# Hybrid mixer and MoE layer: a new order of the mixer's work on four engines

## The reference, cut to what matters

```python
proj = xn @ w_in                       # 1024 -> 1792 columns, 14 column tiles of 128
ya = short_conv_mixer(a_b, a_c, a_x, conv_a_w)          # tiles 0..5
yb = pool_mixer(p_u, pool_w, pool_b, pool_scale)        # tiles 6, 7
yc = s5_mixer(s_u, ...)                                 # tiles 8, 9: bu = B u, h = scan(a, bu), y = C h + d u
yd = rglru_mixer(l_x, l_g, ...)                         # tiles 10..13
branch = einsum('bskw,kwd->bskd', stack(ya, yb, yc, yd), branch_w)
gates  = sigmoid(xn @ merge_gate_w + merge_gate_b)
merged = sum(gates * branch) ;  out = merged @ w_out
```

## Time and profile before

| what | value |
| --- | --- |
| median of 3 runs | 2529.59 us (2528.16 to 2534.01) |
| the profiled execution | 2537.29 us, its span 2535.6 us |
| PE, DVE, ACT, POOL busy in the span | 93%, 54%, 44%, 27% |
| granted TensorE clock, mean | 0.969 of full speed |
| mixer, from the start to the first merge matmul | 500 us |

### The profile page before, as it was taken

How to read it: one execution, slowest core, us unless ns; L and a number is a source line. 1 busy time by engine, 2 the same in 40 slices (tenths; PEclk the granted TensorE clock), 3 DMA queues, 4 the chain that set the end, 5 groups by cost and what they waited for, 6 DMA issues and landing times. The chain is left out here.

```text
span 2535.6 us, 33774 instructions
## 1 busy us (share of the span) xinstructions
PE 2359.7 (93%) x11388; PEld 1854.2 (73%) x11389; DVE 1369.4 (54%) x1967; ACT 1118.1 (44%) x1444; POOL 673.4 (27%) x514
## 2 busy tenths in 40 slices
PE   6979899799999999999999999499999999999991
PEld 5757777688888888888888887377667766677771
DVE  6888575634444444434443444655555556547565
ACT  4523333133333333333333332457666666567673
POOL 3821101100000000000000000077555756567771
PEclk9989999899999999999999999699999999999996
DMA  7864747343354435543463333379777978799987
GB/s 238 321 233 156 240 169 238 89 147 94 106 195 141 125 94 169 179 125 94 119 222 94 100 96 112 141 251 339 276 256 270 340 263 270 261 328 346 328 296 285
DMA packets 311869, 516.31 MB, mean 204 GB/s; under 512 B 33180, under 2 KB 211616, under 8 KB 295392
## 3 DMA queue, kind: packets, MB, share of 16 engines
q1 hardware_dynamic: 295312, 458.17, 51.4%
q0 software_dynamic: 16464, 56.90, 8.9%
HBM read 430.33 MB, written 84.68 MB: 203 GB/s over the span
## 5 line engine op out<-in xcount | busy, mean ns | idle before, releaser
L1496 PE MATMUL mrgps<-xn_hi,w_hi 128*128 128x512 f32 x1024 | 401.4, 392 | 6.7 <-DVE w_lo L1615 6.7
L1496 PE MATMUL mrgps<-xn_hi,w_lo 128*128 128x512 f32 x1024 | 399.5, 390 | 0.0
L1496 PE MATMUL mrgps<-xn_lo,w_hi 128*128 128x512 f32 x1024 | 399.5, 390 | 0.0
L1998 POOL TENSOR_TENSOR w_lo<-w_raw,w_hi 128x1024 fp32r<-128x1024 f32 x128 | 343.0, 2836 | 0.0
L2159 PE MATMUL exps<-w_hi,x_room 128*128 128x512 f32 x1024 | 330.4, 399 | 4.9 <-issue 4.3
L1427 ACT ACTIVATE gt<-mrgps,mb 128x512 f32<-128x512 f32 x128 | 88.3, 690 | 509.1 <-PE mrgps L1496 503.0
L1761 POOL MEMSET x_ident<- 128x128 f32 x1 | 0.2, 205 | 1109.1 <-POOLq L1223 1109.1
L1993 DVE TENSOR_TENSOR w_lo<-w_raw,w_hi 128x2048 fp32r<-128x2048 f32 x126 | 283.5, 2310 | 0.0
L1632 DVE SCALAR_TENSOR_TENSOR tmp<-gt,mrgps 128x512 f32<-128x512 f32 x96 | 66.0, 688 | 387.0 <-PE mrgps L1496 387.0
L1983 ACT ACTIVATE w_hi<-w_raw 128x2048 fp32r<-128x2048 f32 x128 | 239.1, 1921 | 8.4 <-DMA w_raw<-in_expert_w_dram 8.3
L2159 PEld LDWEIGHTS exps<-w_hi,x_room 128*128 128x128 f32 x1024 | 193.2, 189 | 65.1 <-issue 18.3
(11 more groups left out here) (427 smaller groups left out, 4114.5 us busy)
## 6 DMA issues: line engine op xcount, KB each, us to landing
w_raw<-in_expert_w_dram SPq DMA_DIRECT2D x192, 1024.0 KB, 10.1
w_raw<-in_merge_gate_w_dram SPq DMA_DIRECT2D x128, 512.0 KB, 4.0
win_hi<-w_in_parts SPq DMA_DIRECT2D x42, 512.0 KB, 3.6
win_lo<-w_in_parts SPq DMA_DIRECT2D x42, 512.0 KB, 4.9
w_raw<-in_branch_w_dram SPq DMA_DIRECT2D x128, 128.0 KB, 4.1
wout<-in_w_out_dram SPq DMA_DIRECT2D x64, 256.0 KB, 4.5
w_raw<-in_x_dram SPq DMA_DIRECT2D x16, 512.0 KB, 9.7
branch_rows<-in_x_dram SPq DMA_DIRECT2D x16, 512.0 KB, 5.8
```

The source lines that it names most:

```text
L1496: last = pe.matmul(bank[:], w[:, u % 2, kk], x, start=(kk == w_tiles[0] and j == 0), stop=(kk == w_tiles[-1] and j == 2))
L1998: eng.tensor_tensor(self.lo2[:, f], self.raw2[:, f], self.hi2[:, f].bitcast(F32), ALU.subtract).then_inc(self.split2, 1)
```

## The change

The computation is the same. Its parts:
- In chunk 1 `states_in` waits for ACT's copies of `toeplitz` only; the wait for the diagonal stands ahead of `states_out(0, 0)`.
- The order of the steps of chunks 1, 2 and 3 is written anew on PE, DVE and ACT, with tile 9 ahead of `glu(c - 1)` in chunks 2 and 3.
- The transposed x is stored in 4 pieces of 1 MB, each behind another weight load, and x is read in two pairs of pieces in place of four at once; two stores move.
- In chunk 0 the row scales are worked out in two halves (rows 0, 1 and rows 2, 3 of the four x pieces), DVE scales pieces 1 and 3 and ACT pieces 0 and 2, and ACT does the high parts of the first weight pieces later.

```diff
-            return f(*range(6)) + gates(c) + f(6, 7, 8) + glu(c - 1) + f(9, 10, 11) + (glu(c) if c == CH - 1 else [])
+            return f(*range(6)) + gates(c) + f(6, 7, 8, 9) + glu(c - 1) + f(10, 11) + (glu(c) if c == CH - 1 else [])
...
                     if i == 7:
                         store(0, c - 1, ya_full, ya)
+                    if i == (10 if c == 1 else 7):
                         store(1, c - 1, yb_full, pl)
...
-                    if i == 6 and c + 1 < CH:
-                        store_xT(c)
-                        load_x(c + 1)
+                    if 4 <= i < 8 and c + 1 < CH:
+                        store_xT(c, (i - 4,))
+                    if 8 <= i < 10 and c + 1 < CH:
+                        load_x(c + 1, (2 * i - 16, 2 * i - 15))
...
             squares(0)
-            for i in range(2):
-                w_highs(i)
-            scale_rows(0)
+            scale_rows(0, (0, 2))
+            w_highs(0)
             act.wait_ge(g1_in, 16)
-            x_highs(0)
+            x_highs(0, range(2))
+            w_highs(1)
+            x_highs(0, range(2, KD))
             w_highs(2)
...
                 lru_root(c)
                 evac(c, 8)
+                evac(c, 9)
                 glu_tanh(c - 1)
-                evac(c, 9)
...
             pool_out(0)
-            pe.wait_ge(toep_set, 1)
+            pe.wait_ge(toep_copied, 2 * Q)
             states_in(0, 0)
             tile(1, 4)
-            states_in(0, 1)
             tile(1, 5)
             gates(1)
             tile(1, 6)
+            states_in(0, 1)
             tile(1, 7)
+            pe.wait_ge(toep_set, 1)
             states_out(0, 0)
-            states_out(0, 1)
             tile(1, 8)
             tile(1, 9)
+            states_out(0, 1)
+            tile(1, 10)
+            states_in(1, 0)
+            tile(1, 11)
             pool_out(1)
-            states_in(1, 0)
-            tile(1, 10)
+            tile(1, 12)
             states_in(1, 1)
-            for i in range(11, NF):
-                tile(1, i)
+            tile(1, 13)
             glu(0)
...
+                if c == 2:
+                    tile(c, 4)
+                    states_out(c - 1, 1)
...
+                if c == 2:
+                    gates(c)
+                    tile(c, 6)
+                    states_in(c, 0)
+                    tile(c, 7)
+                    states_in(c, 1)
...
                 tile(c, 8)
+                tile(c, 9)
                 glu(c - 1)
-                tile(c, 9)
...
-            rms_scale(s, 0)
-            x_lows(0)
+            for first in (0, 2):
+                rms_scale(s, 0, slice(first, first + 2))
+                row = xin[:, first + 1]
+                dve.tensor_scalar(row, row, rst[:, first + 1:first + 2], None, ALU.mult).then_inc(xh_full, 1)
+            x_lows(0, range(KD))
...
             lru_squares(1)
-            pool_mix(1)
             lru_out(1)
             for u in range(2):
                 y_poly(0, u)
+            pool_mix(1)
...
+            rms_scale(s, 2)
             states(1, 0)
-            rms_scale(s, 2)
-            states(1, 1)
-            conv_a(1, 0)
-            glu_out(0)
...
+                if c == 2:
+                    x_lows(c, range(4))
+                    glu_out(0)
+                    x_lows(c, range(4, KD))
+                    conv_a(1, 0)
+                    conv_a(1, 1)
+                    states(1, 1)
...
                 if c == CH - 1:
+                    pool_mix(c)
                     glu_out(c - 1)
                     for u in range(2):
                         y_poly(c, u)
-                    pool_mix(c)
                     for u in range(2):
                         y_gelu(c, u)
+                    pool_result(c)
                     lru_out(c)
-                    pool_result(c)
```

More of the change, by code:

```diff
@@ L496, in squares, with scale_rows, x_highs @@
                                    accum_out=ssq[:, t:t + 1]).then_inc(sq_done, 1)
[L498 to L500 removed]
+            def scale_rows(c, rows=range(Q)):
+                for t in rows:
+                    act.wait_ge(rst_set, c + 2 if c else t // 2 + 1)
                     act.activation(xin[:, t], xin[:, t], ACT.Copy, scale=rst[:, t:t + 1]).then_inc(xh_full, 1)
[L503 removed]
+            def x_highs(c, ks):
                 if c:
[L505 to L506 removed]
+                    act.wait_ge(xT_out, 64 * c)
+                for k in ks:
                     act.wait_ge(t_full, c * KD + k + 1)
@@ L604, in _ @@
             lru_root(0)
-            x_highs(1)
+            x_highs(1, range(KD))
             for i in range(4):
@@ L644, in _ @@
                     scale_rows(c)
-                x_highs(c)
+                x_highs(c, range(KD))
                 for i in range(4):
@@ L832, in _ @@
                 states_out(c - 1, 0)
-                states_out(c - 1, 1)
-                tile(c, 4)
-                tile(c, 5)
[L836 to L840, removed]
+                if c == 2:
+                    tile(c, 4)
+                    states_out(c - 1, 1)
+                else:
+                    states_out(c - 1, 1)
+                    tile(c, 4)
+                tile(c, 5)
+                if c == 2:
[4 more added lines that the diff above has]
+                    states_in(c, 1)
+                else:
+                    states_in(c, 0)
+                    gates(c)
+                    states_in(c, 1)
+                    tile(c, 6)
+                    tile(c, 7)
                 tile(c, 8)
+                tile(c, 9)
                 glu(c - 1)
-                tile(c, 9)
                 if c == CH - 1:
@@ L855, in _, with rms_scale, x_lows @@
             s = Steps(dve, prep)
[L857 to L861, removed]
+            def rms_scale(steps, c, rows=slice(0, Q)):
+                dve.wait_ge(sq_done, c * Q + rows.stop)
+                steps.link(dve.tensor_scalar(msq[:, rows], ssq[:, rows], 1.0 / D, EPS, ALU.mult, ALU.add))
+                rsqrt_steps(dve, steps, msq[:, rows], rhalf[:, rows], rst[:, rows], rtmp[:, rows])
                 dve.sem_inc(rst_set, 1)
-            def x_lows(c):
+            def x_lows(c, ks):
                 if c == 0:
                     dve.wait_ge(g1_in, 16)
-                for k in range(KD):
+                for k in ks:
                     dve.wait_ge(x_high, c * KD + k + 1)
@@ L1140, in _ @@
             lru_squares(0)
-            x_lows(1)
+            x_lows(1, range(KD))
             pool_mix(0)
@@ L1169, in _ @@
             pool_result(1)
+            rms_scale(s, 2)
             states(1, 0)
-            rms_scale(s, 2)
-            states(1, 1)
-            conv_a(1, 0)
-            glu_out(0)
             for c in range(2, CH):
-                x_lows(c)
-                conv_a(c - 1, 1)
+                if c == 2:
[5 more added lines that the diff above has]
+                    states(1, 1)
+                else:
+                    x_lows(c, range(KD))
+                    conv_a(c - 1, 1)
                 lru_conv(c)
@@ L1184, in _ @@
                 carry_states(c - 1)
-                states(c, 0)
-                gate_poly(c)
+                if c == 2:
+                    gate_poly(c)
+                    states(c, 0)
+                else:
+                    states(c, 0)
+                    gate_poly(c)
                 states(c, 1)
```

18 lines of the change are left out of this document (10 added, 8 removed).

## The result

The changed kernel takes 2507.64 us (median of 4 runs, 2503.71 to 2510.59), the one before in the same runs 2529.88 us. The ratio is 0.9902 (95% interval 0.9889 to 0.9915), 22 us by the medians. The forecast was 2500, with a range of 2486 to 2515.

A forecast was written before the change was run, and what follows sets the result against it. TensorE (PE) is busy 93% of the span, so only its standstills and lower-clock time can be gained. Chunk 0, chunks 1 and 2 together, and chunk 3 gave 0.3 - 14 - 16 = -29.7, from 2529.6 to 2500 us; range 2486 to 2515.

The forecast's parts named there:

- Chunk 0: Start of the mixer: earlier first transpose, but a new 3 to 5 us stop ahead of the fourth tile; +0.3 us.
- Chunk 1, the wait: The 15.2 us stop ahead of states_in(0, 0) and its low clock go: tile 4 done 18 us earlier.
- Chunk 1, the stores: Storing x in 1 MB pieces in chunk 1 costs nothing; without cover, one wait of 3.5 us.
- Chunk 2: Stops of 6 us ahead of glu(1), 4 to 5 ahead of tile 13; chunk 3 starts about 14 us earlier.
- Chunk 3: Three stops (3.9, 3.2, 3.0 us) and their slow stretches go; the merge follows DVE: -16 us.
- no new stops (B): Rival: PE gets no new stops in chunk 2, total 2491 us; chance 0.15.
- all given back (C): Rival: chunk 1's gain ends in chunk 2, only chunk 3's 14 to 16 us stay, 2514 us; chance 0.14.
- Nothing at all (E): Rival: states_in(0, 0) waits for input or bank anyway, the rest trades waits, 2529.6 us; chance 0.05.
- The clock (D): Rival: five shorter stops in chunks 0 to 2 each bring 17 us of low clock, 43 us lost, 2538; chance 0.04.

The follow-up runs named there:

- old_head: The changed kernel with the old chunk 0 (one chain of row scales, ACT scaling all four pieces): 2506.27 us.
- old_wait: The changed kernel with states_in(0, 0) waiting for the diagonal again, every order staying new: 2521.47 us.
- wait_alone: The kernel before with only the wait for the diagonal moved to states_out(0, 0), no order changed: 2529.94 us, ratio 0.9988.
- old_stores: The changed kernel with SP's old order (x stored in two 2 MB pieces, read in four at once, old place of branch B's store): 2512.29 us.
- states_mid: The changed kernel with, in chunk 2, states_in(2, 0) between gates(2) and tile 6 and states_in(2, 1) between tiles 6 and 7: 2498.31 us.
- mid_load: states_mid with SP issuing tile 13's weights ahead of the store of branch C in chunks 2 and 3: 2492.76 us, ratio 0.9848.
- old_chunk3: The changed kernel with the old order of chunk 3 on PE, DVE and ACT: 2520.57 us.

## Why the prediction was right, and where it was not

- **Direction and place** were right: of the forecast 29.7 us, 24.8 and 27.6 are there by the two ratios (0.0098 x 2530 and 0.0109 x 2533), 22.2 and 26.3 by the medians. In the profiles the mixer alone gains 30.7 and 26.8 us, so the sum fits the pair that it was read from and is too large for the other. The weak step is "I take differences within the profile and apply them to the median": PE lost 20.0 us to the low clock in the profiled execution of before and 16.7 in the second, which has no slow stretch behind the pooled sums of chunk 1.
- **Chunk 0**: a stop of 3 to 5 us ahead of the fourth tile was forecast, 5.07 measured; +0.3 forecast, about 0 measured (`old_head`).
- **Chunk 1, the wait**: forecast 18 us for tile 4, 18 to 20 up to the transposes of chunk 2 and 21 to 23 up to its first tile. The two pairs of profiles show 20.8 and 15.5 us up to the transposes, and 24.1 (258.70 to 234.63) and 18.7 up to the first tile; the wait by itself is 14.6 by `old_wait`. This is the term that was mis-sized. Its 3.0 us for the clock behind the stop are 3.0 in the first execution and 1.8 in the second. That the wait needs the order stood nowhere in the prediction; `wait_alone` shows 3 us. The prediction also reads "two waits of 4.6 us" for `x_lows`: there is one, in chunk 2 (4.59); that of chunk 1 is 0.43. Only the one of chunk 2 entered the sum.
- **Chunk 1, the stores**: "I cost it at nothing: its cover is the tile in hand". The nothing was right, since PE has no wait for weights in chunk 1 of the changed kernel. The reason was not: with the old stores the tile in hand didn't cover the load, 4.86 us were missing, and the whole came to 5.4 us (`old_stores`). The gain of the wait was counted in full because the new stores made room for it, and the prediction gave them no part in it, which was luck.
- **Chunk 2**: the stops, 6 and 4 to 5 us forecast, are 6.58 and 2.52; `states(2, 0)` starts at 293.68 (292), `lru_squares(2)` at 315.85 (314), chunk 3 14.3 and 10.3 us earlier (14). `states_mid` and `mid_load` confirm the causes by taking each away: 8.6 and 5.5 us. (The prediction's "17.1" there should be the 16.8 that it had worked out before.)
- **Chunk 3**: -16 forecast, -16.5 and -16.6 in the profiles; 13.7 by the medians of `old_chunk3`, 14.2 in its profile. The other 2 us or so were not taken apart. PE's last `glu` ends at 462.09 and DVE's last step at 465.89, where the prediction's numbers, moved by the 14 us of chunk 2, give 462 and 466.6. (The 40.7 us of PE that it sets "after the gates" are the work behind tile 8.)
- **The range**: its lower end, 2486, is below what its own bounds give (2529.6 - 40 = 2490). Nothing hangs on it here.
- **The rivals**: no new stops (B) is excluded, since chunk 3 is reached at 352.36 and not at 343; all given back (C) too, since no stop of over 8 us stands in chunk 2 or 3. Nothing at all (E) is excluded by the 22 to 26 us; the wait alone would have come near it with 3 us, held by the next set of sums and not by the input or bank of the first. The clock (D): of its five stops three, ahead of the fourth tile, `glu(1)` and tile 13, were followed by a slow stretch, in which PE lost 2.2, 1.7 and 1.7 us, together 5.6, where the sum had 5 and D 43. D priced the stretch by its length, of which a part lies in the stop. The Trainium skill, "TensorE: Matmul & The Clock Gate", section "HAM oscillation — how this bites in real kernels", says that waits between bursts send the array back to the low clock. The rows agree in part: in the changed kernel, behind its start, a slow stretch follows each of the four stops of 2.5 us and more (the fourth is ahead of the merge) and one of 1.88 us, none follows the stops of 1.0 to 1.8 us, and the two executions of before show that the same stop of 2.6 us can have one or not.

## What to carry to other kernels

Taking one wait away is worth what the next instruction on the same engine can do with it: ask who else uses the bank or the queue behind it before you count the stop as gained. The parts don't add up: taking back the wait, chunk 3's order or the stores costs 14.6, 13.7 and 5.4 us, together 33.7, where the whole change brings 26.3. When PE comes earlier, look at the in-order lists of the other engines for a step that waits in front of something needed soon, as the store that held the load of tile 13. And read terms of the clock from two executions, since one may have a slow stretch that the next lacks.

## What the runs showed of the hardware

Behind the same 2.6 us stop the granted clock was 0.57 over 8 us in one execution and 1.00 in another, and PE's loss to the clock in the first 510 us was 20.0 and 16.7 us. The end of the mixer differed by 2.8 us between the two, mostly by this. A shorter stop shows the same: behind the 1.75 us ahead of tile 6 of chunk 2 the clock stayed at 1.00 in both executions of the changed kernel, and in `old_wait` PE lost 1.7 us there at the low clock, from 302 to 306. Why a stop brings a slow stretch in one execution and none in the next was not tried and stays open. At the very start the PEclk of the windows can't be taken as it is: it reads 1.00, but the first eight transposes take 1.94 us in either kernel, against 1.04 for the first eight of chunk 2. Both kernels share this, so no difference rests on it. The slow stretches of the rest of the program (windows of 2 us again, length times what the clock lacks) add up to between 50 and 54 us in every profile of either kernel and of the variants, so the change moved nothing there.
